# A fourth unit by seven products in every second up pair, its buffers out of a smaller descriptor ring, and VectorE operations over two banks

## The reference

```
h = x + 1/2 * SwiGLU_1(RMSNorm(x))             # D_FF = 5632
u = RMSNorm(h);  cols = u @ w_in               # forgetting attention and gated linear attention
merged = sigmoid(gA) * (A @ W_A) + sigmoid(gB) * (B @ W_B)
h = h + merged @ w_out
h = h + 1/2 * SwiGLU_2(RMSNorm(h))
h = h + sigmoid(RMSNorm(h) @ W_pg) * (p @ W_pe)
out = RMSNorm(h)
swiglu(x) = (silu(x @ w_gate) * (x @ w_up)) @ w_down
```

## Time and profile before

| | us |
|---|---|
| median of 3 runs | 2176.55 |
| lowest and highest | 2176.15, 2176.64 |
| the profiled execution | 2176.49 |
| its span (first to last instruction) | 2174.8 |

### The profile page before, as it was taken

One profiled execution on the slowest core, in us unless ns is written; L12 is line 12 of the kernel. 1 busy time (PEld: TensorE's weight loads), 2 busy tenths in 40 slices (PEclk: granted clock), 3 DMA queues, 4 the chain that ended last, 5 costly groups with the idle time before them and its releaser, 6 DMA issues.

```text
span 2174.8 us, 24585 instructions
## 1 busy us (share of the span) xinstructions
PE 2159.9 (99%) x9936; PEld 1777.2 (82%) x9936; DVE 1683.3 (77%) x1750; ACT 1151.3 (53%) x1188; POOL 39.3 (2%) x71
## 2 busy tenths in 40 slices
PE   9999999999999999999999999999999999999998
PEld 7888888888888888878888888888888888888886
DVE  5898889988887877345666665889888998888755
ACT  6554555554555564455444554555555555455554
POOL 0000000000000000110100000000000000000000
PEclk9999999999999999999999999999999999999999
DMA  8555655665565655566665555655565565565464
GB/s 317 217 183 194 230 187 183 206 214 184 190 216 171 222 195 184 169 184 175 182 178 170 186 185 184 240 187 189 194 225 183 193 221 189 195 211 196 143 215 145
DMA packets 140754, 425.79 MB, mean 196 GB/s; under 512 B 10440, under 2 KB 10448, under 8 KB 126304
## 3 DMA queue, kind: packets, MB, share of 16 engines
q1 hardware_dynamic: 138592, 418.68, 57.3%
q0 software_dynamic: 1472, 4.70, 0.9%
q10 hardware_dynamic: 576, 0.82, 0.1%
HBM read 422.06 MB, written 2.11 MB: 195 GB/s over the span
## 4 chain that ended last, share of the span: by engine, by line
PE 92%; DVE 5%; issue 1%; ACT 1%; DMA 0%; SPq 0%; POOLq 0%; POOL 0%; DVEq 0%; ACTq 0%
PE acc L1691 11%; PE acc L1693 11%; PE acc L1692 11%; PE turn L1691 11%; PE turn L1692 10%; PE turn L1693 10%; PE acc L1641 8%; PE acc L1643 8%; PE acc L1642 8%; DVE w_lo L1202 1%; PE turn L1661 1%; DVE raw_r L1202 1%; DVE more_r L1202 1%; ACT more_r L760 0%; PE acc L1669 0%
## 5 line engine op out<-in xcount | busy, mean ns | idle before, releaser
L1145 DVE TENSOR_TENSOR w_lo<-raw,w_hi 128x1024 fp32r<-128x1024 f32 x211 | 264.8, 1261 | 239.5 <-ACT w_hi L703 239.0
L703 ACT ACTIVATE w_hi<-raw 128x1024 fp32r<-128x1024 f32 x211 | 223.2, 1061 | 284.1 <-PE acc L1643 259.1
L1641 PE MATMUL acc<-w_hi,x_both 128*128 128x512 f32 x512 | 203.9, 398 | 0.0
L1643 PE MATMUL acc<-w_hi,x_both 128*128 128x512 f32 x512 | 199.8, 390 | 0.0
L1642 PE MATMUL acc<-w_lo,x_both 128*128 128x512 f32 x512 | 199.4, 389 | 0.0
L760 ACT ACTIVATE w_hi<-raw 128x2048 fp32r<-128x2048 f32 x61 | 117.2, 1922 | 85.5 <-DVE more L1216 21.6
L760 ACT ACTIVATE more_r<-lo_raw 128x2048 fp32r<-128x2048 f32 x63 | 120.6, 1921 | 73.6 <-DVE more L1216 37.2
L1202 DVE TENSOR_TENSOR raw_r<-raw,w_hi 128x2048 fp32r<-128x2048 f32 x61 | 139.4, 2288 | 16.2 <-ACT w_hi L760 15.8
L1202 DVE TENSOR_TENSOR w_lo<-lo_raw,more_r 128x2048 fp32r<-128x2048 f32 x63 | 143.7, 2287 | 8.8 <-ACT more_r L760 8.4
L760 ACT ACTIVATE more_r<-raw 128x2048 fp32r<-128x2048 f32 x55 | 105.4, 1921 | 68.2 <-DVE more L1216 38.0
L760 ACT ACTIVATE w_hi<-lo_raw 128x2048 fp32r<-128x2048 f32 x52 | 99.6, 1920 | 59.0 <-DVE more L1216 29.1
(11 more groups left out here) (433 smaller groups left out, 5518.7 us busy)
## 6 DMA issues: line engine op xcount, KB each, us to landing
lo_raw<-in_ffn_up SPq DMA_DIRECT2D x46, 1024.0 KB, 4.8
raw<-in_ffn_up SPq DMA_DIRECT2D x44, 1024.0 KB, 4.9
raw<-in_w_merge_gate SPq DMA_DIRECT2D x64, 512.0 KB
raw<-in_ffn_w_down SPq DMA_DIRECT2D x24, 1024.0 KB, 5.0
more<-in_ffn_up SPq DMA_DIRECT2D x21, 1024.0 KB, 4.8
lo_raw<-in_ffn_w_down SPq DMA_DIRECT2D x21, 1024.0 KB, 5.0
raw<-in_ffn_up SPq DMA_DIRECT2D x38, 512.0 KB, 3.8
raw<-in_w_in SPq DMA_DIRECT2D x36, 512.0 KB, 3.7
```

Of the source, the lines that this page charges most:

```text
L703: nc.scalar.activation(w_hi[:, slot, :, :], raw[:, slot, :, :], ACT.Copy).then_inc(hi_split, 1)
L1145: nc.vector.tensor_tensor(w_lo[:, slot, :, :], raw[:, slot, :, :], w_hi[:, slot, :, :].bitcast(F32), ALU.subtract).then_inc(lo_split, 1)
L1641: nc.tensor.matmul(to, hi(kt)[:, tok], w_hi[:, slot, k, :], start=kt == 0, stop=False)
L1643: last = nc.tensor.matmul(to, lo(kt)[:, tok], w_hi[:, slot, k, :], start=False, stop=kt == BK * nb - 1)
```

## The change

An up pair with odd n takes four shared units, one with even n three (`US` is now a table, and `shared_units` takes one off for even n). The stages of those pairs run B0 S4 B1 S5 B2 B3 S6 and then the A; the stages before them have A0 A1 A2 A3. A fourth trio of buffers and one more pair of token sums lie in `spare`, 10 KB a partition, made free by `dynamic_dma_scratch_size=4096`. Since the first stage makes the sums of four units, a make and a split are added there at k = 5 and 6. `hidden_out` takes two operations of 512 columns (two banks) in place of four of 256, `combine` one over two banks in place of two, `add_rows` one in place of two. Unit 1's sum for the first two down parts moves from the stage two ahead to the stage just ahead (k = 1 and 2), and the last unit's there by one k (3 and 4). In the second half the turn of the first rows moves from k = 3 to 4 in stage 16. ScalarE's list is moved in the same way as VectorE's, which is shown.

```diff
-US, HS = 3, 3
+US = {"up": 4, "mix": 3}
+TRIOS, HS = 4, 3
...
-    return down_shared(PAIR[ffn][i].part) if PAIR[ffn][i].kind == "down" else US
+    pair = PAIR[ffn][i]
+    if pair.kind == "down":
+        return down_shared(pair.part)
+    return US[pair.kind] - (pair.kind == "up" and pair.n % 2 == 0)
...
+def sums_end(ffn, i):
+    return 4 if shared_units(ffn, i + 1) == HS else 3
...
-    counts, steps, stages, after = {"raw": [0] * TALL, "trio": [0] * US}, 0, {}, {}
+    counts, steps, stages, after = {"raw": [0] * TALL, "trio": [0] * TRIOS}, 0, {}, {}
...
-        quad_free, trio_free = [b0 - 2, b0, early, early], [early] * US
+        quad_free, trio_free = [b0 - 2, b0, early, early], [early] * TRIOS
...
-                    trio = min((t for t in range(US) if t not in held),
+                    trio = min((t for t in range(TRIOS) if t not in held),
...
+        spare, spare_r = shared(("spare", [P, 5, COLS], F32), ("spare_r", [P, 5, COLS], F32R))
...
+            if trio == 3:
+                return ((spare, spare_r)[split][:, 2:5, :],)
...
-        s_hi = room_r[:, 0:3, :].rearrange("p u (s c) -> p u s c", s=4)
-        s_lo = room_r[:, 3:6, :].rearrange("p u (s c) -> p u s c", s=4)
+        s_hi = [*[room_r[:, u, :] for u in range(3)], spare_r[:, 0, :]]
+        s_lo = [*[room_r[:, 3 + u, :] for u in range(3)], spare_r[:, 1, :]]
...
-            return (hid_hi[:, u], hid_lo[:, u]) if PAIR[name][pair].kind == "down" else (s_hi[:, u], s_lo[:, u])
+            if PAIR[name][pair].kind == "down":
+                return hid_hi[:, u], hid_lo[:, u]
+            return tuple(s[u].rearrange("p (s c) -> p s c", s=4) for s in (s_hi, s_lo))
...
             def hidden_out(name, pair):
 
-                banks = banks_of(name, pair)
-                for ct in range(2):
-                    silus[0] += 1
-                    dve.wait_ge(silu_done, silus[0])
-                    for t in range(TT):
-                        part = scratch[:, t, ct * TOK:(ct + 1) * TOK]
-                        last = nc.vector.scalar_tensor_tensor(out=part, in0=banks[2 * ct + t][:, TOK:], scalar=rstd[:, t:t + 1],
-                                                              in1=part, op0=ALU.mult, op1=ALU.mult)
-                    last.then_inc(read_out, 1)
+                silus[0] += 2
+                dve.wait_ge(silu_done, silus[0])
+                for t in range(TT):
+                    part = scratch[:, t, :].rearrange("p (n c) -> p n c", n=2)
+                    last = nc.vector.scalar_tensor_tensor(out=part, in0=set_of(name, pair)[:, t::2, TOK:], scalar=rstd[:, t:t + 1],
+                                                          in1=part, op0=ALU.mult, op1=ALU.mult)
+                last.then_inc(read_out, 2)
...
@@ -1222,9 +1233,10 @@
                 last_added[0] = ADDED[name, pair]
                 dve.wait_ge(parts_copied, ADDED[name, pair])
                 c11, c21, c12, c22 = banks_of(name, pair)
+                c21_c12 = set_of(name, pair)[:, 1:3, :]
                 after_own(nc.vector.tensor_tensor(m1_copy, c22[:, :], m1_copy, ALU.add))
-                nc.vector.tensor_tensor(c12[:, :], c12[:, :], m1_copy, ALU.add)
-                after_own(nc.vector.tensor_tensor(c21[:, :], c21[:, :], m1_copy, ALU.add))
+                both = room[:, 6:7, :].to_broadcast([P, 2, COLS])
+                after_own(nc.vector.tensor_tensor(c21_c12, c21_c12, both, ALU.add))
                 nc.vector.tensor_tensor(c22[:, :], c21[:, :], m5_copy, ALU.add).then_inc(combined, 1)
...
@@ -1258,16 +1270,14 @@
 
             def add_rows(c, banks, factor):
 
-                for t in range(TT):
-                    rows = h[:, t, COLS * c:COLS * (c + 1)]
-                    last = nc.vector.scalar_tensor_tensor(out=rows, in0=banks[t][:, :], scalar=factor,
-                                                          in1=rows, op0=ALU.mult, op1=ALU.add)
-                last.then_inc(read_out, 1)
+                rows = h[:, :, COLS * c:COLS * (c + 1)]
+                nc.vector.scalar_tensor_tensor(out=rows, in0=banks, scalar=factor, in1=rows, op0=ALU.mult, op1=ALU.add)\
+                    .then_inc(read_out, 1)
...
                             dve.wait_ge(multiplied, it.at)
-                            add_rows(3, banks_of(name, LAST_DOWN)[2:4], 0.5)
+                            add_rows(3, set_of(name, LAST_DOWN)[:, 2:4, :], 0.5)
...
                             for ct in range(2):
-                                add_rows(2 * FFN[i - 1].n + ct, banks_of(name, i - 1)[2 * ct:2 * ct + 2], 0.5)
+                                add_rows(2 * FFN[i - 1].n + ct, set_of(name, i - 1)[:, 2 * ct:2 * ct + 2, :], 0.5)
...
-                        if (n == 0 or i == LAST_DOWN + 1) and 3 <= k <= 5:
+                        if (n == 0 or i == LAST_DOWN + 1) and 0 <= k - 3 < US[PAIR[name][i + 1].kind]:
                             split_sums(name, i + 1, k - 3)
-                        if (n == 0 or i == LAST_DOWN + 1) and 2 <= k <= 4:
+                        if (n == 0 or i == LAST_DOWN + 1) and 0 <= k - 2 < US[PAIR[name][i + 1].kind]:
                             make_sums(name, i + 1, k - 2, hi, lo)
...
@@ -1312,24 +1322,24 @@
                             make_sums(name, i + 2, 0)
                         if i + 1 in LAST_UP and k == sum_made_at(i) + 1:
                             split_sums(name, i + 2, 0)
-                        if i + 1 in LAST_UP and k == sum_made_at(i) + 3 and shared_units(name, i + 2) == HS:
-                            make_sums(name, i + 2, 1)
-                        if i in LAST_UP and k == 2:
+                        if i in LAST_UP and shared_units(name, i + 1) == HS and k == 1:
+                            make_sums(name, i + 1, 1)
+                        if i in LAST_UP and shared_units(name, i + 1) == HS and k == 2:
+                            split_sums(name, i + 1, 1)
+                        if i in LAST_UP and k == sums_end(name, i) - 1:
                             u = shared_units(name, i + 1) - 1
                             make_sums(name, i + 1, u, slab_r[:, 0:HID, :], slab_r[:, HID:2 * HID, :])
-                        if i + 1 in LAST_UP and k == sum_made_at(i) + 4 and shared_units(name, i + 2) == HS:
-                            split_sums(name, i + 2, 1)
-                        if i in LAST_UP and k == 3:
+                        if i in LAST_UP and k == sums_end(name, i):
                             split_sums(name, i + 1, shared_units(name, i + 1) - 1)
-                        if i == LAST_DOWN and k == 3:
-                            if p_turn:
-                                turn_plain(TURN["p"], TURN["p"] % 2, p_hi, p_lo)
+                        if i == LAST_DOWN and k == 3 and p_turn:
+                            turn_plain(TURN["p"], TURN["p"] % 2, p_hi, p_lo)
+                        if i == LAST_DOWN and k == (4 if p_turn else 3):
                             turn_rows("down" + name[-1], 0, next_hi, next_lo, gain)
                         if i == LAST_DOWN and k == 5:
                             turn_rows("down" + name[-1], 1, next_hi, next_lo, gain)
                     if i == LAST_DOWN:
                         dve.wait_ge(half_done, 1 if name == "ffn1" else 2)
-                        add_rows(2, banks_of(name, LAST_DOWN)[0:2], 0.5)
+                        add_rows(2, set_of(name, LAST_DOWN)[:, 0:2, :], 0.5)
...
                                 last = plain_part(name, it, ct, *operand, primed)
-                            last.then_inc(multiplied, 1)
+                            last.then_inc(multiplied, item_counts(name, it))
...
-    nc = bacc.Bacc("TRN2", target_bir_lowering=False, num_devices=1)
+    nc = bacc.Bacc("TRN2", target_bir_lowering=False, num_devices=1, dynamic_dma_scratch_size=4096)
```

More of the change, by code:

```diff
@@ L253, in sum_number @@
         downs = sum(down_shared(part) for part in range(len(PARTS)))
-        first = (US + downs + US) * (name == "ffn2")
+        first = (US["up"] + downs + US["mix"]) * (name == "ffn2")
         if PAIR[name][pair].kind == "up":
@@ L257, in sum_number @@
         if PAIR[name][pair].kind == "mix":
-            return first + US + downs + u
-        return first + US + sum(down_shared(n) for n in range(PAIR[name][pair].part)) + u
+            return first + US["up"] + downs + u
+        return first + US["up"] + sum(down_shared(n) for n in range(PAIR[name][pair].part)) + u
     x_tm = x[0].rearrange("(t p) d -> p t d", p=P)
@@ L414, in build @@
         tall_full = [sem(f"tall_full{i}") for i in range(TALL)]
-        trio_full = [sem(f"trio_full{i}") for i in range(US)]
+        trio_full = [sem(f"trio_full{i}") for i in range(TRIOS)]
         steps_made, parts_copied, combined = sem("steps_made"), sem("parts_copied"), sem("combined")
@@ L1259, in add_rows @@
             def add_rows(c, banks, factor):
-                for t in range(TT):
-                    rows = h[:, t, COLS * c:COLS * (c + 1)]
```

(8 more changed lines are left out.)

2 lines of the change are left out of this document (1 added, 1 removed).

## The result

The changed kernel takes 2197.55 us (median of 4 runs, 2197.05 to 2199.48), the kernel before, run beside it, 2176.38 (2176.15 to 2176.64). The ratio is 1.0099, with a 95% interval of 1.0087 to 1.0111: slower by 1.0%. The forecast was 2198.4.

A forecast was written before the change was run, and what follows sets the result against it. TensorE, busy 99%, was taken as the bound, made late by the order of VectorE's work. Matmuls -6.1 and waits 30.9 in place of 2.9 (+28.0) gave net +21.9 on 2176.49: 2198.4 us, range 2187 to 2210.

The forecast's parts named there:

- Matmuls, -6.1: TensorE in the nine odd up pairs' units: 27 matmuls fewer at 0.2267 us each, 6.1 us saved.
- Stages of the kind of 7, three times 2.0: Stage 7 in both halves, stage 1 in the second: TensorE starts A1 at 30.05, not 28.07; 2.0 us lost each.
- Stages 3 and 9, four times 2.9: Both halves: two sums on VectorE, working without pause from 1.85 us; waits 1.4 at S6, 1.5 at A1, 11.7 in all.
- Stage 13, twice 3.1: Both halves: as stage 7, with the next down pair's sum behind the subtractions; 3.1 us lost each, 6.2 in all.
- Stages 2 and 8, four times 0.8 for 0.5 before: Both halves: moved sum frees 1.89 us, fourth A comes in; 0.8 us lost at A2 where 0.5 was, 3.1 in all.
- Second half's first stage, 3.9: The fourth sum adds 2.62 us on VectorE and A3 comes on top; TensorE loses 3.9 us by A2.
- the clock falls: Rival, chance 0.04: TensorE runs 12 matmuls behind each of some 14 waits at 1.2 GHz, +38 us, 2237.
- First half's stage 1, 0: The fourth sum's 2.62 us meet a slack of 2.2, without an A3: 0.4 at most, taken as nothing.
- Reordered turn of the first rows, 0: Second half, stage 16, k 3 to 4: lies where VectorE idles, so no change in time.
- Combining and sums of rows, 0: VectorE's operations over two banks: between 0.06 us gained and 0.3 lost, taken as no change.
- Loads and GpSimd's ring, 0: No term in the sum; rivals: late loads in nine stages with four A, 2205, chance 0.09; full ring, 2205, chance 0.03.
- VectorE keeps up: Rival, chance 0.08: A1's split in the odd pairs' nine stages is done 28.1 us in, so faster, 2170.

The follow-up runs named there:

- the third experiment: Against the changed kernel, in stages with four B the turned hidden values are subtracted one item later, behind the split of B3: 2189.89 us, ratio 1.0062.

## Why the prediction was right, and where its terms were off

- **Matmuls, -6.1**: 27 fewer, as counted.
- **Stages of the kind of 7, three times 2.0**: 2.0 to 2.1 lost. The reason given, VectorE held back by the turned values, is shown by the third experiment.
- **Stages 3 and 9, four times 2.9** (1.4 at S6, 1.5 at A1): 3.1, in two waits of 1.4 and a little in the matmuls behind each. The amount of work was right. Of it 0.5 us belong to an edit that I had priced at no change: from 1.85 us on was counted for products that wait for all four silus, and that this waiting was itself part of the change, and dear, I did not see.
- **Stage 13, twice 3.1**: 3.2 (2.8 more than before).
- **Stages 2 and 8, four times 0.8 for 0.5 before**: 0.7 to 0.8.
- **Second half's first stage, 3.9** (A1 1.7, A2 2.1): waits of 1.63 and 2.14. In one experiment without a clock fall the stage takes 59.43, that is 6.6 over before, less 2.7 for the A: 3.9. In the changed kernel's profile the clock fell behind the second wait, 1.6 us more. This is the rival "the clock falls", in one of its some fourteen places; I had it at 2.7 a place, for 12 matmuls at the lower level, and about eight ran at it. So one of the forecast's own signs of being wrong, a granted clock under 1.00, did come, in this stage alone; the sum had no term for it.
- **First half's stage 1, 0**: 52.54 for 52.55.
- **Reordered turn of the first rows, 0**: it gained 1.1 us. In the second half TensorE waited there for a split that stood behind the turn on VectorE. Before, then after:

```profile
2055.08 0.47 PE L1691 MATMUL acc<-more_r,slab_r 128*128 128x512 f32 x1 [1.32 <-DVE more_r L1202]
```

```profile
2078.07 0.47 PE L1701 MATMUL acc<-more_r,slab_r 128*128 128x512 f32 x1 [0.18 <-DVE more_r L1213]
```

  I had looked at VectorE's idle time in that stage and not at the item that waits. The wait of 1.3 us stood in the list of TensorE's waits.
- **Combining and sums of rows, 0**: within the spread. They take 1.23 and 1.22 us for 1024 columns over two banks.
- **Loads and GpSimd's ring, 0**: TensorE's 24 waits end with VectorE's splits alone. Loads do come late for VectorE, as that rival had it, but in other places: ahead of the steps of a fourth A in stages 6 and 12 of both halves, 6.1 us in four waits, where TensorE waits for nothing. The longest:

```profile
303.89 0.69 DVE L1224 TENSOR_TENSOR more<-more 128x512 f32<-128x512 f32 x1 [1.57 <-DMA spare<-in_ffn_up]
```

  That the smaller ring costs something elsewhere was not tried by itself; the kernel with three units, which has it, is faster than before.

In sum, the stages lose 33.2 us to waits and slow matmuls where 30.9 were forecast: 31.6 to waits, 1.6 to the clock. That in place of 2.9, less 6.1 of matmuls and 1.2 at both ends of the kernel (the turn's 1.1 among it), is 23.0 of a measured 22.9 in the span. The waits were right stage by stage; that the sum came out within 1.0 is in part luck, since the clock's 1.6, which it left out, and the turn's 1.1, which it had at nothing, nearly cancel. The other three runs are no nearer to the forecast of 2198.4 on the whole: 2198.02 is 0.4 off, 2197.07 and 2197.05 1.3, the profiled one 1.1. Their granted clock over the whole kernel is 0.999 and not 0.998, so they may have had no fall; no trace of them was read.

The rival "VectorE keeps up" is out for the reason given against it: VectorE's share of stage 3 is 94%, not all of it, and it is still late, because a cheap item for TensorE (12 matmuls, 2.7 us) is a dear one for VectorE (4.86 us), and three or four of them stand in a row at the end of the stage.

## What to carry to other kernels

When an algorithm trades matmuls for element-wise work, don't compare the engines' shares: walk the row of items and count, at each, how far the slower engine has come and when TensorE gets there; here the waits followed to 0.2 us in a stage of 42, and to 0.7 us in the sum of 31. Put the trade where the helper engine can work ahead, that is where nothing it must first wait for stands in its queue: the same fourth unit lost some 30 us of waiting in the odd pairs and nothing behind a down pair. And when operations are merged, look at what each of them waits for: the merged one waits for the last of all.

## What the runs showed of the hardware

**The granted clock falls after some waits of some 2 us, not after all.** TensorE behind the wait for A2 in the second half's first stage, in the changed kernel, and the same place in the kernel with unit 1's sum back:

```profile
1420.19 0.51 PE L1701 MATMUL turn<-w_hi,y_r 128*128 128x512 f32 x1 [1.85 <-DVE more_r L1213]
1420.52 0.60 PE L1702 MATMUL turn<-more_r,y_r 128*128 128x512 f32 x1
1420.92 0.63 PE L1703 MATMUL turn<-w_hi,y_r 128*128 128x512 f32 x1
1421.35 0.63 PE L1701 MATMUL turn<-w_hi,room_r 128*128 128x512 f32 x1
...
1423.91 0.42 PE L1701 MATMUL turn<-w_hi,room_r 128*128 128x512 f32 x1
```

```profile
1420.13 0.50 PE L1701 MATMUL turn<-w_hi,y_r 128*128 128x512 f32 x1 [1.85 <-DVE more_r L1213]
1420.47 0.39 PE L1702 MATMUL turn<-more_r,y_r 128*128 128x512 f32 x1
1420.70 0.39 PE L1703 MATMUL turn<-w_hi,y_r 128*128 128x512 f32 x1
```

From one matmul to the next 0.43 us (1420.92 to 1421.35) in place of 0.23: the lower of the two levels, 1.2 in place of 2.4 GHz, until 1423.91, while TensorE is at work without a pause. The wait before is the same, 1.85 us by the profile and 2.0 from start to start beyond a matmul's 0.23, in both. The profiled executions of the changed kernel and of the experiments have 18 waits of this length (1.80 to 1.85 us in the profile), with a fall behind 8: in 4 of 10 places in the kernel with B apart, in 0 of 5 in the kernel with unit 1's sum back, and in the one place each in the changed kernel, the one with the turned values later and the two with operations bank by bank. Counting the kernel with B apart too, this place, behind A2's wait, had a fall in five executions of six. In the changed kernel and the one with B apart each fall cost 1.6 us. No wait of 1.7 us or less in any stage had one. What decides between two equal waits is open. The Trainium skill, "TensorE: Matmul & The Clock Gate" (Part 1), says that the throttled clock is the default and that activity releases it. The trace agrees in that each of the 8 falls comes right behind a wait; why the other ten waits had none, that sentence doesn't tell.

**Two PSUM banks in one operation.** Over 2x512 columns the combining takes 1.23 us and the sum of rows 1.22, each time, as one of 1024 columns in SBUF does (1.22). So a second bank costs no second start here. The Trainium skill's "VectorE: DVE Perf Modes" (side-by-side) has 150 cycles of start, 8 to fill the pipe and one element a cycle at 0.96 GHz; an estimate from these for 1024 elements is 1.23 us, and the trace agrees. The rows:

```profile
L1239 DVE TENSOR_TENSOR acc<-acc,room x17: 1232/1233/1233, 100.7 to 2057.1; 128x1024 f32<-128x1024 f32 x17
L1274 DVE SCALAR_TENSOR_TENSOR h<-acc,h x16: 1214/1218/1225, 235.0 to 2092.2; 128x1024 f32<-128x1024 f32 x16
```
